# Gate rows of a two-block transformer kernel from fp32 products in column groups

## What is computed

```python
def _mixer(h, lb, w_in, b_in, ...):
    z = h @ w_in + b_in                      # h = rms(x) * g, 512 x 1024
    (a_q, a_k, a_v, a_f, b_qk, b_v, b_i, b_f, b_o, c_q, c_f, c_i, c_g) = _split_cols(z)
    ...
    ca = jnp.cumsum(jax.nn.log_sigmoid(a_f.astype(f32)), axis=1).transpose(0, 2, 1)
    oa = _fox_attention(qa, ka, _heads(a_v, A_HEADS), ca)
    ...
    ob = _mlstm_chunkwise(..., b_i.astype(f32).transpose(0, 2, 1), b_f.astype(f32).transpose(0, 2, 1))
```

## Time and profile before

| | |
|---|---|
| time, median of 3 runs | 1093.35 us (1092.87 to 1093.53) |
| span of the profiled execution, first to last instruction | 1091.2 us |
| lies around the span, against the median | 2.15 us |
| PE busy | 1078.4 us, 99% |
| DVE busy | 713.4 us, 65% |
| ACT busy | 421.6 us, 39% |

### The profile page before, as it was taken

How to read it: one execution, slowest core, us unless ns; L and a number is a source line. 1 busy time by engine, 2 the same in 40 slices (tenths; PEclk the granted TensorE clock), 3 DMA queues, 4 the chain that set the end, 5 groups by cost and what they waited for, 6 DMA issues and landing times.

```text
span 1091.2 us, 13622 instructions
## 1 busy us (share of the span) xinstructions
PE 1078.4 (99%) x5409; PEld 868.7 (80%) x5411; DVE 713.4 (65%) x1142; ACT 421.6 (39%) x663; POOL 0.2 (0%) x4
## 2 busy tenths in 40 slices
PE   9999999999999999999999999999999999999997
PEld 6877877877878888888888888887776777888886
DVE  6897877868768887754488745654568446364431
ACT  6612555334352323222222234744357443323232
POOL 0000000000000000000000000000000000000000
PEclk9999999999999999999999999999999999999999
DMA  8432121131213223233422134333121222033302
GB/s 256 121 116 78 39 77 41 57 136 39 78 39 126 97 97 106 58 87 101 151 78 87 49 97 154 92 102 116 44 78 39 78 77 78 1 117 115 111 25 77
DMA packets 100240, 95.94 MB, mean 88 GB/s; under 512 B 5953, under 2 KB 91089, under 8 KB 100177
## 3 DMA queue, kind: packets, MB, share of 16 engines
q1 hardware_dynamic: 100000, 95.05, 27.2%
q10 hardware_dynamic: 176, 0.02, 0.0%
HBM read 92.95 MB, written 2.10 MB: 87 GB/s over the span
## 4 chain that ended last, share of the span: by engine, by line
PE 94%; DVE 3%; ACT 1%; issue 1%; DVEq 0%; ACTq 0%
PE ring L1031 23%; PE ring L1033 22%; PE ring L1032 22%; PE bank L1031 3%; PE bank L1033 3%; PE bank L1032 3%; PE bank L1486 1%; PE bank L1281 1%; PE bank L1253 1%; PE bank L1186 1%; PE bank L1266 1%; PE bank L1118 1%; PE bank L1510 1%; PE bank L1459 1%; PE ring L1349 1%
## 5 line engine op out<-in xcount | busy, mean ns | idle before, releaser
L1031 PE MATMUL ring<-act_hi,w_hi 128*128 128x512 f32 (+1 forms) x816 | 323.5, 396 | 0.9 <-DVE xT L2302 0.5
L1033 PE MATMUL ring<-act_hi,w_lo 128*128 128x512 f32 (+1 forms) x816 | 316.7, 388 | 0.0
L1032 PE MATMUL ring<-act_lo,w_hi 128*128 128x512 f32 (+1 forms) x816 | 316.4, 388 | 0.0
L1574 ACT ACTIVATE w_hi<-w_raw 128x2048 fp32r<-128x2048 f32 (+4 forms) x97 | 160.9, 1659 | 248.1 <-PE ring L1033 212.8
L1918 DVE TENSOR_TENSOR w_lo<-w_raw,w_hi 128x2048 fp32r<-128x2048 f32 (+5 forms) x102 | 191.4, 1879 | 4.0 <-ACT w_hi L1574 3.7
L1031 PEld LDWEIGHTS ring<-act_hi,w_hi 128*128 128x128 f32 x816 | 153.3, 188 | 37.4 <-issue 3.9
L1032 PEld LDWEIGHTS ring<-act_lo,w_hi 128*128 128x128 f32 x816 | 153.3, 188 | 31.8 <-issue 1.9
L1033 PEld LDWEIGHTS ring<-act_hi,w_lo 128*128 128x128 f32 x816 | 153.2, 188 | 31.7
L1033 PE MATMUL ring<-hidH,w_lo 128*128 128x512 f32 x176 | 68.5, 389 | 0.0
L1031 PE MATMUL ring<-hidH,w_hi 128*128 128x512 f32 x176 | 68.5, 389 | 0.0
L1032 PE MATMUL ring<-hidL,w_hi 128*128 128x512 f32 x176 | 68.5, 389 | 0.0
(11 more groups left out here) (360 smaller groups left out, 1624.4 us busy)
## 6 DMA issues: line engine op xcount, KB each, us to landing
w_raw<-in_w_in SPq DMA_DIRECT2D x30, 1024.0 KB, 5.1
w_raw<-in_w_up SPq DMA_DIRECT2D x22, 1024.0 KB, 5.0
w_raw<-in_w_out SPq DMA_DIRECT2D x8, 1024.0 KB, 5.0
w_raw<-in_w_down SPq DMA_DIRECT2D x8, 768.0 KB, 4.6
w_raw<-in_w_down SPq DMA_DIRECT2D x8, 640.0 KB, 4.3
w_raw<-in_w_in SPq DMA_DIRECT2D x7, 512.0 KB, 5.8
xin<-in_xt SPq DMA_DIRECT2D x8, 256.0 KB, 4.2
xT<-in_xt SPq DMA_DIRECT2D x2, 1024.0 KB, 6.6
```

What stands on the lines that cost most here:

```text
L1031: pe.matmul(out, ah, bh, start=(first and n == 0), stop=False)
L1032: pe.matmul(out, ah, bl, start=False, stop=False)
L1033: mm = pe.matmul(out, al, bh, start=False, stop=(last and n == len(pairs) - 1))
L1574: return act.activation(out, src, func, **more)
```

## The change

The chunk of gate weights, its split and the 24 products go. In their place:

- SP loads one table `wgate` (128 x 352, fp32) at the program's start, behind the parameters: eight blocks of 32 columns (16 used), and a selector of 96 columns of zeros and ones. DVE multiplies the 256 weight columns by the norm's gain, in stage x_rs.
- Stage `gate_parts`, at the tile's old place: eight plain fp32 products of the unsplit input `xin` with 32 weight columns each. Product k writes to rows 32 (k mod 4) and on of bank 4, so that each of four column groups sums two of the eight blocks. They wait for `gate_dve` to reach 2 (the scaled weights, and DVE's copy rs_xcol of bank 4). DVE then multiplies the four sums by rsx into `gpart` (128x512).
- Stage `gates`, now behind cb_a 0: one fp32 product of the selector with `gpart` adds the four groups and puts the rows to 0, 32 and 64. It waits for `gate_dve` to reach 3, which is the multiply into `gpart`. DVE's drain adds the bias, so ACT's pass over gz goes, and gate_ln stands behind this drain.
- Chunk numbers fall by one: cb0 is chunk 2, cb1 chunk 3, b_qk0 chunk 4 (the one put by hand).

```diff
-        chunk("gates", w_gate_d)
...
         products(2)
-        in_tile("gates", 0, "gates")
+        stage("gate_parts")
         products(1)
-        stage("gate_ln")
...
         for b in range(NB):
             stage("cb_a", b)
+            if b == 0:
+                tile(("gates", 0))
+                stage("gates", 0)
+                stage("gate_ln")
             fill_slot()
...
+            sp.dma_start(wgate[:], w_gate_d).then_inc(par_in, 16)
...
+                elif kind == "gate_parts":
+
+                    pe.wait_ge(gate_dve, 2)
+                    for k in range(KD):
+                        c = 32 * (k % 4)
+                        mm = pe.matmul(bank[4][c:c + 32, :], wgate[:, 32 * k:32 * k + 32], xin[:, k, :], start=(k < 4), stop=(k >= 4))
+                    mm.then_inc(x_col, 1)
                 elif kind == "gates":
-                    channels(s, kind, 0, act)
+                    out = open_bank(s)
+                    pe.wait_ge(gate_dve, 3)
+                    pe.matmul(out[0:96, :], wgate[:, KD * 32:], gpart[:], start=True, stop=True).then_inc(tile_done, 1)
...
-                elif kind == "gates":
-                    act.wait_ge(bank_free(s), drains(s))
-                    A(gz[:], gz[:], ACT.Identity, bias=pc("b_gate", r=slice(0, 96))).then_inc(z_in, 1)
...
+                elif kind == "gate_parts":
+
+                    dve.wait_ge(x_col, 2)
+                    TT(gpart[:], bank[4][:], rsx[:], ALU.mult).then_inc(gate_dve, 1)
                 elif kind == "gates":
 
                     dve.wait_ge(tile_done, upto(s))
-                    TT(gz[:], at_ring(s)[0:96, :], rsx[0:96, :], ALU.mult).then_inc(bank_free(s), 1)
+                    TS(gz[:], at_ring(s)[0:96, :], pc("b_gate", r=slice(0, 96)), None, ALU.add).then_inc(bank_free(s), 1)
...
-                    CP(rs_xcol, bank[4][:, 0:NB]).then_inc(dve_step, 1)
-                    dve.wait_ge(dve_step, step())
+                    CP(rs_xcol, bank[4][:, 0:NB]).then_inc(gate_dve, 1)
+                    dve.wait_ge(gate_dve, 2)
                 elif kind == "x_rs":
-                    dve.wait_ge(par_in, 16)
...
+                    dve.wait_ge(par_in, 32)
...
+                    wg = wgate[:, 0:KD * 32].rearrange("p (k n) -> p k n", n=32)
+                    TT(wg, wg, wide(pc("g_mix", 0, KD), 32), ALU.mult).then_inc(gate_dve, 1)
```

More of the change, by code:

```diff
@@ L125, in two_blocks @@
         zeros_ready = sem("zeros_ready")
+        gate_dve = sem("gate_dve")
         x_sq, x_sum, x_ss, x_rs, x_hi, x_lo, x_col, z_in = (
             sem(n) for n in ("x_sq", "x_sum", "x_ss", "x_rs", "x_hi", "x_lo", "x_col", "z_in"))
-        lb_d, lb_e, nbcf_ready, mask_ready = (sem(n) for n in ("lb_d", "lb_e", "nbcf_ready", "mask_ready"))
+        lb_nbcf, lb_e, mask_ready = (sem(n) for n in ("lb_nbcf", "lb_e", "mask_ready"))
         gate_ln, gate_m, gate_rows, gate_cols, negC_ready, negB_in = (
@@ L223, in two_blocks @@
         g3 = sb("g3", [96, T], F32, M + 106.75)
+        gpart = sb("gpart", [P, T], F32, M + 104.75)
+        wgate = sb("wgate", [P, KD * 32 + 96], F32, M + 106.75)
         negC = sb("negC", [8, T], F32, M + 108.75)
@@ L886, in two_blocks @@
                 z_at[s[1:]] = len(z_at) + 1
-            elif s[0] in ("gates", "b_qk", "c_g", "b_o", "a_q", "a_k"):
+            elif s[0] in ("b_qk", "c_g", "b_o", "a_q", "a_k"):
                 z_at[s] = len(z_at) + 1
@@ L1609, in _ @@
                     A(rsx[:], rsx[:], ACT.Exp, scale=-0.5).then_inc(x_rs, 1)
-                    act.wait_ge(lb_d, 1)
+                    act.wait_ge(lb_nbcf, 1)
                     A(lbe, lbd, ACT.Exp).then_inc(lb_e, 1)
@@ L1613, in _ @@
                     p = s[2]
-                    act.wait_ge(nbcf_ready, 1)
+                    act.wait_ge(lb_nbcf, 2)
                     act.wait_ge(bank_free(s[1:]), drains(s[1:]))
@@ L1628, in _ @@
                     A(bo[:, s[1], :], bo[:, s[1], :], ACT.Sigmoid, bias=pc("b_bo", s[1])).then_inc(z_in, 1)
-                elif kind == "gates":
-                    act.wait_ge(bank_free(s), drains(s))
-                    A(gz[:], gz[:], ACT.Identity, bias=pc("b_gate", r=slice(0, 96))).then_inc(z_in, 1)
                 elif kind == "gate_ln":
-                    act.wait_ge(z_in, z_at["gates", 0])
+                    act.wait_ge(bank_free(("gates", 0)), drains(("gates", 0)))
                     A(g1[:], gz[:], ACT.Abs).then_inc(act_step, 1)
@@ L1971, in _ @@
                     dve.wait_ge(x_col, 1)
-                    CP(rs_xcol, bank[4][:, 0:NB]).then_inc(dve_step, 1)
-                    dve.wait_ge(dve_step, step())
+                    CP(rs_xcol, bank[4][:, 0:NB]).then_inc(gate_dve, 1)
+                    dve.wait_ge(gate_dve, 2)
                 elif kind == "x_rs":
-                    dve.wait_ge(par_in, 16)
-                    TT(lbd, pc("lb", 0, 2), pc("lb", 0, 2), ALU.subtract).then_inc(lb_d, 1)
-                    TS(nbcf, pc("b_cf", 0, 2), -1.0, None, ALU.mult).then_inc(nbcf_ready, 1)
+                    dve.wait_ge(par_in, 32)
+                    TT(lbd, pc("lb", 0, 2), pc("lb", 0, 2), ALU.subtract).then_inc(lb_nbcf, 1)
+                    TS(nbcf, pc("b_cf", 0, 2), -1.0, None, ALU.mult).then_inc(lb_nbcf, 1)
+                    wg = wgate[:, 0:KD * 32].rearrange("p (k n) -> p k n", n=32)
+                    TT(wg, wg, wide(pc("g_mix", 0, KD), 32), ALU.mult).then_inc(gate_dve, 1)
                 elif kind == "params":
@@ L2094, in _ @@
                         dve.wait_ge(hg_a_used, n - 5)
-                    if n == 2:
-                        dve.wait_ge(tile_done, upto(("gates", 0)))
                     q64 = cq[:].rearrange("p h c t -> p (h c) t")
@@ L2610 @@
     cols("b_fconv", a["ffn_conv_b"][0])
-    w_gate = _np.zeros((P, KD, P), _np.float32)
-    for row, at, n in ((0, OFF_AF, AH), (32, OFF_BI, BH), (64, OFF_BF, BH)):
-        w_gate[:, :, row:row + n] = w_in[:, at:at + n].reshape(KD, P, n).transpose(1, 0, 2)
+    w_gate = _np.zeros((P, KD * 32 + 96), _np.float32)
+    for row, at, n, col in ((0, OFF_AF, AH, 0), (32, OFF_BI, BH, 8), (64, OFF_BF, BH, 12)):
+        w_gate[:, 0:KD * 32].reshape(P, KD, 32)[:, :, col:col + n] = w_in[:, at:at + n].reshape(KD, P, n).transpose(1, 0, 2)
         par[row:row + n, PCOL["b_gate"][0]] = b_in[at:at + n]
+        for i in range(n):
+            w_gate[col + i::32, KD * 32 + row + i] = 1.0
     lam = _np.concatenate([a[f"diff_lambda_{v}_2"][0] for v in ("q1", "k1", "q2", "k2")])
```

## The result

The changed kernel takes 1100.31 us (median of 5 runs, 1099.4 to 1101.06) against 1093.35 us (1092.79 to 1093.53, 5 runs): ratio 1.0064, 95% interval 1.0052 to 1.0076, 7.0 us more. The forecast was 1100.8. The profiled execution took 1099.71 us, its span (first to last instruction) is 1097.9 us.

What follows compares the result with a forecast made beforehand. PE's own queue was taken to bound the kernel nearly everywhere. Stall +4.8 and clock +2.7 made 7.5 us on a span of 1091.2, so 1098.7; with 2.15 around the span 1100.8 us, range 1097.2 to 1102.4.

Steps and rivals of the forecast that it cites:

- What bounds: Whole kernel: PE is the bound nearly everywhere, busy 1078.4 of 1091.2 us, so its own queue sets the time.
- The shift stays as it is to the end: Behind the first hg_win: all that follows keeps its distances to PE, so nothing comes back later.
- The sum: Whole kernel: +4.8 for the stall and +2.7 for the clock, 7.5 us on a span of 1091.2.
- The 2.15 us around the span: Time outside the first-to-last-instruction span, against the median of 1093.35; added to 1098.7 to give 1100.8 us.
- The eight products: Narrow products in gate_parts: four column groups run together, two rounds of 0.86, 1.72 us plus 0.1 on each side.
- The first wait: PE at gate_parts waits for DVE's copy rs_xcol: ready at 30.08, the eight products start at 31.07.
- The second wait: PE's selector behind cb_a 0 waits for the multiply into gpart, idle from 35.8 to 42.2: +4.8 us.
- The multiply: DVE's multiply into gpart, queued behind hg_begin and two steps, runs from 41.42 for 0.69 us.
- The clock: PE's clock drops to half in the 6.4 us gap at the selector: +2.7 us behind it, bounds 0 and 3.5.
- The cover on DVE: DVE's new work ahead of the drain at 26.83 ends at 26.5, hidden by an old gap, 0.3 us to spare.
- Rival (a): Same stall at the selector, but the clock holds, by luck or groups filling the gap: +4.8, 1098.1 us; chance 0.16.
- Rival (b): The multiply into gpart doesn't hold PE at the selector: no gap, no clock drop, -1.55, 1091.8 us; chance 0.04.

Runs made afterwards that it cites:

- e1: The changed kernel with DVE's multiply into gpart moved ahead of hg_begin, PE's order unchanged: 1091.8 us.
- e5: The changed kernel with the selector, gz's drain and gate_ln moved behind cb_a 3 instead of cb_a 0, DVE's multiply left in place: 1091.49 us.
- e4: The changed kernel with DVE's multiply into gpart moved between hg_begin and the first hg_att step: 1097.14 us.
- e2: The changed kernel with 26 bf16 products of zeros in PE's gap between cb_a 0 and the selector, the wait left as it is: 1097.18 us.
- e3_one_group: The changed kernel with all eight narrow products in one column group, multiply and selector on these 32 rows alone: 1099.39 us.
- e9_one_late: e5 with all eight narrow products in one column group, as in e3_one_group: 1097.03 us.

## Why the prediction was right, step by step

- **What bounds.** Right as far as PE's queue goes: it sets the time, and what was lost at hg_win is still lost at 677 us. "The shift stays as it is to the end" is wrong twice: 0.6 us more go at the norm, and 0.9 come back in the last stores, which the forecast had no term for. The two traces give 6.84 at hg_win, then +0.6, +0.1 in small steps and -0.9, which is 6.6 us at the end. That +6.84 and the median's +6.96 agree so well is luck in part: two terms that nobody foresaw nearly cancel.
- **The sum.** Forecast 7.5 us more; measured 6.7 in the span (1097.9 against 1091.2, the 6.6 and a shift of 0.1 from before x_col on) and 7.0 in the median. The 2.15 us around the span were too many: time and span differ by 1.7 to 1.9 us in every execution for which both are listed, and the rest was the profiled execution's distance from the median.
- **The eight products.** Forecast 1.72 + 0.1 on either side; measured 31.18 to 33.03, 1.85. The inference from two groups to four held (3.7 times). By the Trainium skill ("TensorE: Matmul & The Clock Gate", Part 3), whose 2.38 times is for three tiles, it would have been an estimated 2.2 us; the measurement decides.
- **The first wait.** Forecast from 30.08 to 31.07, measured 0.86 us to 31.18.
- **The second wait.** Forecast 6.4 us with the selector at 42.2; measured 6.26 and 42.30. The multiply: forecast 41.42, measured 41.46. e1 and e5 show that it is the distance between the two places; in e4 the gap shrinks by as much as the multiply moved (2.7 us). Forecast +4.8, measured +4.72 (e2).
- **The clock.** The mechanism was right and the size too large: forecast +2.7, measured 2.1 (6.84 - 4.72). The term was sized by the start of the program, 5.94 us at the low level; here PE worked at it from 42.30 to 46.65, 4.35 us, and half of that is 2.2. The start was no good measure of it: the clock had fallen near 40 and was at the low level for a part of the gap already, where it costs nothing. That the start ran at the lower level was read off its 0.44 us a product, since the granted clock shows 1.00 there; the 0.43 us at a granted 0.50 here bear it out.
- **The cover on DVE.** Forecast 0.3 us to spare ahead of the drain, measured 0.51.
- **Rival (a)** was worked out wrongly in one part. It had the clock hold when the gap is filled by products in turn; e3_one_group did just that and the clock fell all the same, 1099.39 and not 1098.1. Its other path to 1098, a gap by luck without a fall, was in neither of two traces nor in the 5 runs (lowest 1099.4; the mean granted clock of each is 0.997).
- **Rival (b)** named the gap ahead of hg_begin as the only place for the multiply that would turn the sign, at 1091.8 us. e1_mul_early put it there: 1091.8.

## What to carry to other kernels

An engine that comes to wait for a result that only a side engine used to wait for inherits that result's whole queue: before a product is put behind a small vector operation, read off the trace when the vector engine gets to that place, not how long the operation takes (here 0.69 us against 6.3 of wait). If PE must wait, the price is the gap and the lower clock behind it (1.5 us behind a gap of 3.6, 2.1 and 2.3 behind one of 6.3). The cure adds no work: move either end, the small operation into a gap of its engine or the product behind work that has its operands.

## What the runs showed of the hardware

- Four column groups of 128 rows by 32 columns run fp32 products of 512 columns at the same time: eight in 1.92 us, against 7.05 in one group.
- TensorE's granted clock fell to half near 40 us in a gap of 6.3 us, and near 39 in one of 3.6 us; the low level lasted for 4.35 us of work after the first and about 2.8 after the second. In e3_one_group it fell too, after 7 us of narrow products, 3 us of full ones, 1.1 us of idle time and 2 us of work; without the idle stretch (e9_one_late) it stayed at 1. In e2_keep_warm 5.56 us of bf16 products of zeros in the gap held it.
- The last two stores of 256 KB took a median of 2.9 us with a load of instructions (one packet, 0.01 MB) among them, in three traces, and 2.2 without, in eleven.
